# The first loads in parts, the second tile's transposes inside the first chunk, and 26 small products ahead of them

## The chip, the cores and the metric

The kernel runs on one core of a Trainium2 chip. TensorE (PE in the rows, with PEld for its weight loads) does the matrix products and transposes, VectorE (DVE), ScalarE (ACT) and GpSimd (POOL) work on their results, and SyncE (SP) issues nearly all the DMAs. The metric is device time in microseconds for one whole execution, the median of several runs. All data are 32-bit floats.

## What is computed

The reference is two transformer blocks in a row over 256 tokens of 1024 numbers: four layers of one kind, then two of another with experts. What matters here is the very first operation on `x`, the projection of layer 0, and the memory's norm beside it:

```
def first_block(x, mem, ...):
    mem_n = layer_norm(mem, mem_ln_g, mem_ln_b)
    for i in range(DEPTH):
        if kind == 0:
            q, k, v, qi, wi, ki, qm = split_cols(x @ w_in_a[j], ...)
            ki = apply_rope(layer_norm(ki, ...))
            mix = dsa_attention(q, k, v, qi, wi, ki)
        ...
        mk, mv = jnp.split(mem_n @ w_mem_kv[i], 2, axis=-1)
```

`x @ w_in_a[0]` is 256 x 1024 times 1024 x 3144. Everything else in the kernel comes after it.

## The kernel before

The 256 tokens are two tiles of 128 rows (`x[:, 0, :]` and `x[:, 1, :]`). A product takes an activation transposed to 128 x 128 blocks (`xT`) as its stationary operand and a stretch of weights, up to 512 columns wide, as its moving operand. A product of 32-bit numbers shows in the trace as two records, each with a weight load of its own; a transpose is one record.

Weights stream through `ring`, 12 slots of 1 MB each. SP issues loads in the order of the program text; `slot()` makes it wait until the slot's last user is counted in `slots_used`, and each load counts up `slot_full[s]`. The projection is cut into chunks of columns (`FIRST_CHUNKS`): the first is 512 wide (columns 2304 to 2815), the second 328, the third 512. A 512-wide chunk is two slots: rows 0 to 511 of the weights and rows 512 to 1023, which is `k` = 0 to 3 and `k` = 4 to 7 of the eight 128-row blocks.

SP's program (L690 to L697) begins with `ident` (the identity for the transposes), `x` tile 0, `x` tile 1, the two slots of the first chunk, then the memory rows `memrows`, the causal mask, two small constants, and from there the second chunk on. Nothing holds these back but the issue itself: the first wait for a free slot comes at the thirteenth.

TensorE's program for this part is: wait for `ident` and tile 0 (`x_loaded`), eight transposes of tile 0, wait for tile 1, eight of tile 1, each four of them (`transposes`, L994) into one of two PSUM banks `trp`, from which ScalarE copies them to `xT` (L2058). Then `linear_chunk` for each chunk: for each slot, four products of tile 0 and four of tile 1 into two banks of `lin` (L827 is the helper that issues every product), and a count on `slots_used` after each slot. ScalarE copies the finished pair of banks out (L2049). The third chunk has the transposes of the normalised memory between its quarters (`memory_columns`), which wait on `ln_done` from VectorE; VectorE's norm of the memory starts when the gain and bias (`in_mem_ln_g`, `in_mem_ln_b`) have landed. VectorE's first instruction is a memset of `ones` (L3435), which counts up `dve_step`.

In the rows, `sco` is another pair of PSUM banks, first used by the index scores of layer 0.

Of the kernel before, what the change touches and what calls it, by code (L numbers as in the profile page):

```python
# [15 lines left out]
P = 128  # L16
D = 1024
SEQ = 256
NT = SEQ // P
KD = D // P  # L20
# [6 lines left out]
HEADS, DH = 12, 64  # L27
# [36 lines left out]
SLOT = 2048  # L64
# [110 lines left out]
class Tally:  # L175
# [10 lines left out]
    def next(self, k=1):  # L186

        self.n += k
        return self.value()
# [32 lines left out]
def build(nc, A, out):  # L222
    ctx = ExitStack()
    with ctx:
        def sem(name):
            return ctx.enter_context(nc.semaphore(name))
# [199 lines left out]

        slot_full = [sem(f"slot_full{s}") for s in range(X_PLACE + 1)]
        slots_used = sem("slots_used")
        x_loaded, second_tile_loaded, input_loaded = sem("x_loaded"), sem("second_tile_loaded"), sem("input_loaded")
        proj_done = sem("proj_done")  # L430
        tr_full, tr_done = sem("tr_full"), sem("tr_done")
# [117 lines left out]
        def _(sp):  # L549
# [16 lines left out]
            def load_chunk(w, c, n, per=4):  # L566
                K = w.shape[0]
                per = min(per, K // P)
                for k in range(0, K // P, per):
                    load(slot(), 0, per * n,  # L570
                         w[k * P:(k + per) * P, c:c + n].rearrange("(k p) n -> p k n", p=P))
# [116 lines left out]

            sp.dma_start(ident[:, :], const("ident")).then_inc(x_loaded, 16)  # L690
            sp.dma_start(x[:, 0, :], A["x"][0, 0:P, :]).then_inc(x_loaded, 16)
            sp.dma_start(x[:, 1, :], A["x"][0, P:2 * P, :]).then_inc(second_tile_loaded, 16)
            load_chunk(A["w_in_a"][0], *FIRST_CHUNKS[0][0])
            sp.dma_start(memrows, A["mem"][0].rearrange("(t p) d -> p t d", p=P)).then_inc(input_loaded, 16)
            sp.dma_start(causal[:, :, :].rearrange("p t k -> p (t k)"), const("causal")).then_inc(input_loaded, 16)
            sp.dma_start(inv_freq, const("inv_freq")).then_inc(input_loaded, 16)
# [94 lines left out]
        def _(pe):  # L791
# [23 lines left out]
            def slot(loads=1):  # L815
                s = place[0] % RING
                place[0] += 1
                pe.wait_ge(slot_full[s], full[s].next(16 * loads))
                return s
# [123 lines left out]
            def linear_chunk(srcT, K, n, after_each=None, fresh=False):  # L943

                kt = K // P
                per = min(4, kt)
                pair = 2 * (lin_items[0] % 2)
                lin_items[0] += 1
                if t_proj.due():
                    pe.wait_ge(proj_done, t_proj.value())  # L950
                for k0 in range(0, kt, per):
                    s = slot()
                    w = ring[:, s, 0:per * n].rearrange("p (k n) -> p k n", k=per)
                    for t in range(NT):
                        if fresh and (k0 == 0 or t == NT - 1):
                            await_transposes(0 if k0 else (3, 1)[t])
                        for k in range(per):
                            last = mm(lin[:, pair + t, 0:n], srcT[:, k0 + k, t * P:(t + 1) * P], w[:, k, :],
                                      start=k0 + k == 0, stop=k0 + k == kt - 1)
                        if t == NT - 1:  # L960
                            last.then_inc(slots_used, 1)
                        if after_each is not None:
                            after_each()
# [23 lines left out]
            def transposes(pieces, free_slots=0):  # L987

                b = tr_items[0] % 2
                tr_items[0] += 1  # L990
                if t_tr.due():
                    pe.wait_ge(tr_done, t_tr.value())
                for j, src in enumerate(pieces):
                    ins = nc.tensor.transpose(trp[0:src.free_size(), b, j * P:(j + 1) * P], src, ident[:, :])  # L994
                    if j == len(pieces) - 1:
                        ins.then_inc(tr_full, 1)
                    elif free_slots:
                        ins.then_inc(slots_used, 1)
                        free_slots -= 1
                assert not free_slots  # L1000
# [844 lines left out]
                combine_half(1)  # L1845
                t_y.skip(2 * NT)

            pe.wait_ge(x_loaded, 16 * 2)
            for t in range(NT):
                if t:  # L1850
                    pe.wait_ge(second_tile_loaded, 16)
                for b in range(0, KD, 4):
                    transposes([x[:, t, (b + j) * P:(b + j + 1) * P] for j in range(4)])
            for layer in range(FIRST_LAYERS):
                kind = kind_of(layer)
                proj = projA if kind == 0 else projBC
# [1 line left out]
                widths = [n for _, n in FIRST_CHUNKS[kind]]  # L1858
                if layer == 0:
                    memory_left = memory_columns()  # L1860
                    for c, n in enumerate(widths[:3]):
                        linear_chunk(xT, D, n, (lambda: next(memory_left)) if c == 2 else None, c == 0)
                    hold(2)
                    for _ in memory_left:
                        pass
                    linear(memT, D, 512, True)
                else:
                    await_transposes()
                    linear_by_tile(xT, D, widths[:2], lambda: x_columns(1, 1))
                    linear_chunk(xT, D, widths[2])  # L1870
# [1716 lines left out]
```

## Time and profile before

| | us |
|---|---|
| median of 3 runs | 2934.1 |
| lowest and highest | 2932.8, 2934.61 |
| the profiled execution | 2932.43 |
| its span, first to last instruction | 2930.6 |

The profiled execution is 1.7 us below the median. TensorE is busy for 89% of the span. The rows below are from this one execution; times in them are microseconds from the start of the span unless marked ns. In a timeline row the first number is the start, the second the stretch covered, then the engine, the line, the operation, what is written and read, the count of instructions merged in it, and in brackets how long the engine was idle before and what released it.

### The profile page before, as it was taken

How to read it: one execution, taken by the hardware profiler on the slowest of the kernel's cores; microseconds unless marked ns; L12 is line 12 of the kernel's file. 1: busy time of each engine (PE TensorE's matmuls, PEld its weight loads, DVE VectorE, ACT ScalarE, POOL GpSimd, SP SyncE). 2: the span in 40 equal slices, each digit the busy share in tenths (PEclk: the TensorE clock that was granted, in tenths of full speed). 3: DMA queues.
4: the chain of work that ended last, by engine and by line, in shares of the span. 5: the costliest groups of instructions: out<-in, count | busy, mean ns of one | idle time of the engine just before them, and what ended most of it. 6: DMA issues, size and time to landing. Idle time of an engine off the chain costs nothing.

```text
span 2930.6 us, 36560 instructions
## 1 busy us (share of the span) xinstructions
PE 2594.1 (89%) x15534; PEld 1596.4 (54%) x15534; DVE 1193.0 (41%) x2460; ACT 393.7 (13%) x736; POOL 219.9 (8%) x218
## 2 busy tenths in 40 slices
PE   8999999999999999999998999666668999766665
PEld 4569745895559944698457664222224665222221
DVE  2667625675166744777465103001002533100111
ACT  1410002100131001300022111000000412000000
POOL 1110012000120001200011000000000310000000
PEclk9999999999999999999997999878888999888888
DMA  8344543543535435354424557999999455999998
GB/s 310 115 146 165 179 143 112 188 172 136 194 102 187 175 132 172 102 181 178 136 83 146 187 206 280 421 421 421 422 421 379 144 213 183 421 421 421 422 421 342
DMA packets 243719, 703.50 MB, mean 240 GB/s; under 512 B 18795, under 2 KB 119657, under 8 KB 195171
## 3 DMA queue, kind: packets, MB, share of 16 engines
q1 hardware_dynamic: 242256, 699.30, 63.3%
q8 instruction: 126, 2.06, 0.3%
q10 hardware_dynamic: 1299, 1.83, 0.2%
q14 instruction: 38, 0.31, 0.0%
HBM read 698.20 MB, written 1.05 MB: 239 GB/s over the span
## 4 chain that ended last, share of the span: by engine, by line
PE 69%; DMA 21%; SPq 3%; issue 3%; DVE 2%; ACT 1%; POOL 0%; DVEq 0%; POOLq 0%; ACTq 0%
PE lin L827 44%; PE sco L827 14%; PE trp L827 9%; DMA ring<-in_moe_w_up 4%; DMA ring<-in_moe_w_gate 4%; DMA arena<-in_moe_w_down 3%; DMA ring<-in_moe_w_down 3%; DMA spare<-in_moe_w_gate 3%; SPq L663 3%; DMA spare<-in_moe_w_down 2%; PE trp L994 1%; DMA spare<-in_moe_w_up 1%; DMA arena<-in_moe_w_gate 1%; PE trp L1082 1%; DMA ring<-in_xa_wkv 0%
## 5 line engine op out<-in xcount | busy, mean ns | idle before, releaser
L827 PE MATMUL lin<-ring,arena 128*128 128x512 f32 (+4 forms) x2244 | 825.9, 578 | 18.7 <-DMA ring<-in_moe_w_down 8.8
L827 PEld LDWEIGHTS lin<-ring,arena 128*128 128x128 f32 (+1 forms) x2244 | 359.5, 177 | 396.4 <-issue 379.7
L827 PE MATMUL sco<-ring,arena 128*32 128x512 f32 (+2 forms) x1380 | 308.4, 812 | 170.9 <-DMA ring<-in_moe_w_up 52.3
L827 PE MATMUL lin<-arena 128*128 128x128 f32 (+9 forms) x2984 | 356.4, 355 | 28.8 <-DMA arena<-in_moe_w_down 11.2
L827 PE MATMUL sco<-arena 128*32 128x512 f32 (+7 forms) x1832 | 304.8, 457 | 72.9 <-DMA ring<-in_moe_w_gate 26.3
L3350 DVE TENSOR_TENSOR arena<-arena,sco 128x512 f32<-128x512 f32 x16 | 11.0, 688 | 723.7 <-PE sco L827 723.7
L827 PEld LDWEIGHTS lin<-arena 128*128 128x128 f32 (+4 forms) x2984 | 227.0, 162 | 124.1 <-issue 103.8
L827 PEld LDWEIGHTS sco<-ring,arena 128*32 128x32 f32 (+1 forms) x1380 | 84.5, 150 | 339.5 <-issue 337.3
L827 PEld LDWEIGHTS sco<-arena 128*32 128x32 f32 (+4 forms) x1832 | 142.2, 164 | 190.3 <-issue 185.5
L2502 POOL TENSOR_TENSOR roots<-roots 128x1 f32<-128x1 f32 (+2 forms) x42 | 59.7, 1423 | 2332.7 <-DVE roots L2613 2302.7
L827 PE MATMUL lin<-arena,ring 128*128 128x128 f32 (+2 forms) x1672 | 226.6, 301 | 0.0
L827 PE MATMUL trp<-arena 128*128 128x128 f32 (+2 forms) x1520 | 218.1, 299 | 0.6 <-DVE arena L3330 0.6
L827 PEld LDWEIGHTS lin<-arena,ring 128*128 128x128 f32 (+1 forms) x1672 | 207.2, 188 | 14.6 <-issue 3.6
L827 PEld LDWEIGHTS trp<-arena 128*128 128x128 f32 (+1 forms) x1520 | 176.7, 191 | 40.4 <-issue 40.4
L827 PE MATMUL sco<-arena,ring 128*128 128x128 f32 (+1 forms) x1172 | 139.4, 275 | 2.2 <-DVE arena L3282 1.4
L827 PEld LDWEIGHTS sco<-arena,ring 128*128 128x128 f32 x1172 | 135.2, 192 | 5.5 <-DVE arena L3282 3.1
L827 PE MATMUL sco<-spare,arena 128*32 128x512 f32 (+2 forms) x224 | 117.3, 677 | 7.5 <-DMA ring<-in_moe_w_gate 6.0
L2827 DVE TENSOR_TENSOR arena<-ring 128x512 f32<-128x512 f32 x132 | 88.1, 694 | 71.3 <-PE sco L827 70.4
L2058 ACT ACTIVATE arena<-trp 128x512 f32<-128x512 f32 (+1 forms) x115 | 63.2, 590 | 372.5 <-PE trp L994 372.4
L2831 DVE TENSOR_TENSOR ring<-ring 128x512 f32<-128x512 f32 x132 | 89.0, 701 | 1.5
L827 PE MATMUL lin<-spare,arena 128*128 128x512 f32 (+1 forms) x184 | 86.1, 614 | 3.2 <-DMA ring<-in_moe_w_down 3.2
L2833 DVE TENSOR_TENSOR arena<-ring,arena 128x512 f32<-128x512 f32 x132 | 87.8, 692 | 0.0
(337 smaller groups left out, 2285.0 us busy)
## 6 DMA issues: line engine op xcount, KB each, us to landing
ring<-in_w_gate_up SPq DMA_DIRECT2D x88, 1024.0 KB, 5.4
ring<-in_moe_w_up SPq DMA_DIRECT2D x87, 1024.0 KB, 26.7
ring<-in_moe_w_gate SPq DMA_DIRECT2D x75, 1024.0 KB, 27.0
arena<-in_moe_w_down SPq DMA_DIRECT2D x57, 1024.0 KB, 27.0
ring<-in_moe_w_down SPq DMA_DIRECT2D x53, 1024.0 KB, 27.3
ring<-in_w_down SPq DMA_DIRECT2D x44, 1024.0 KB, 5.3
arena<-in_moe_w_gate SPq DMA_DIRECT2D x40, 1024.0 KB, 23.0
arena<-in_moe_w_up SPq DMA_DIRECT2D x31, 1024.0 KB, 27.0
```

Of the source, the lines that this page charges most:

```text
L663: sp.dma_start(dst, src).then_inc(slot_full[s], 16)
L827: return nc.tensor.matmul(o, lhsT, rhs, start=start, stop=stop, skip_group_check=not one_group)
L994: ins = nc.tensor.transpose(trp[0:src.free_size(), b, j * P:(j + 1) * P], src, ident[:, :])
L1082: last = nc.tensor.transpose(trp[:, e, to:to + P], pair_P[j % 3][:, e, lo:lo + P], ident[:, :])
L2058: nc.scalar.activation(dst, trp[0:rows, b, 0:n].rearrange("p (a b) -> p a b", a=shape[1]), ACT.Copy, scale=scale).then_inc(tr_done, 1)
L2502: nc.gpsimd.tensor_tensor(root_out[:, b, 0:n], root_in[:, b, 0:n], root_power[:, 0:n], ALU.pow).then_inc(root_done, 1)
L2827: V.tensor_tensor(first, w12, w11, ALU.subtract).then_inc(dve_step, 1)
L2831: V.tensor_tensor(w12, w22, w12, ALU.subtract)
L2833: ins = V.tensor_tensor(second, w22, first, ALU.subtract)
L3350: V.tensor_tensor(pair_h, pair_silu, sco[:, 1, :], ALU.mult).then_inc(h_done, 1)
```

## The change

SP's first loads are split and put in another order; TensorE's first chunk is written out by hand. In words:

- Tile 0 of `x` comes in two halves of 512 columns, with a semaphore for each (`x_loaded`, `x_rest_loaded`).
- The first weight slot comes in two halves of two row blocks, the first of them (`first_weights_loaded`) ahead of tile 1 of `x`, the second behind it. Two more DMAs are issued than before; the bytes are the same.
- TensorE first waits for VectorE's memset of `ones` and then does 26 products of `ones` with `ones`, 64 columns out of 64, into `sco`; nobody reads them.
- The eight transposes of tile 0 follow, in two groups of four, each behind its half. Then two products of tile 0 (k = 0, 1), the eight transposes of tile 1, two products of tile 0 (k = 2, 3), four of tile 1, and the second slot as before.

```
-            sp.dma_start(x[:, 0, :], A["x"][0, 0:P, :]).then_inc(x_loaded, 16)
+            sp.dma_start(x[:, 0, 0:512], A["x"][0, 0:P, 0:512]).then_inc(x_loaded, 16)
+            sp.dma_start(x[:, 0, 512:D], A["x"][0, 0:P, 512:D]).then_inc(x_rest_loaded, 16)
+            first_column, first_width = FIRST_CHUNKS[0][0]
+            first_rows = [A["w_in_a"][0][256 * h:256 * h + 256, first_column:first_column + first_width].rearrange("(k p) n -> p k n", p=P)
+                          for h in range(2)]
+            s = slot()
+            sp.dma_start(ring[:, s, 0:1024].rearrange("p (k n) -> p k n", k=2), first_rows[0]).then_inc(first_weights_loaded, 16)
             sp.dma_start(x[:, 1, :], A["x"][0, P:2 * P, :]).then_inc(second_tile_loaded, 16)
-            load_chunk(A["w_in_a"][0], *FIRST_CHUNKS[0][0])
+            load(s, 1024, SLOT, first_rows[1])
+            load(slot(), 0, SLOT, A["w_in_a"][0][512:D, first_column:first_column + first_width].rearrange("(k p) n -> p k n", p=P))
...
-            pe.wait_ge(x_loaded, 16 * 2)
-            for t in range(NT):
-                if t:
-                    pe.wait_ge(second_tile_loaded, 16)
+            def first_chunk(n):
+
+                def product(t, k):
+                    return mm(lin[:, t, 0:n], xT[:, k, t * P:(t + 1) * P], w[k // 4][:, k % 4, :], start=k == 0, stop=k == KD - 1)
+
+                def input_columns(t, b):
+                    transposes([x[:, t, (b + j) * P:(b + j + 1) * P] for j in range(4)])
+
+                t_proj.due()
+                lin_items[0] += 1
+                pe.wait_ge(dve_step, 1)
+                for _ in range(26):
+                    mm(sco[0:DH, 0, 0:DH], ones[:, :], ones[:, :])
+                pe.wait_ge(x_loaded, 16 * 2)
+                input_columns(0, 0)
+                pe.wait_ge(x_rest_loaded, 16)
+                input_columns(0, 4)
+                w = [ring[:, s, 0:4 * n].rearrange("p (k n) -> p k n", k=4) for s in range(2)]
+                pe.wait_ge(first_weights_loaded, 16)
+                await_transposes(1)
+                for k in range(2):
+                    product(0, k)
+                pe.wait_ge(second_tile_loaded, 16)
                 for b in range(0, KD, 4):
-                    transposes([x[:, t, (b + j) * P:(b + j + 1) * P] for j in range(4)])
+                    input_columns(1, b)
+                assert slot() == 0
+                for k in range(2, 4):
+                    product(0, k)
+                await_transposes(1)
+                for k in range(4):
+                    last = product(1, k)
+                last.then_inc(slots_used, 1)
+                assert slot() == 1
+                for k in range(4, KD):
+                    product(0, k)
+                await_transposes()
+                for k in range(4, KD):
+                    last = product(1, k)
+                last.then_inc(slots_used, 1)
...
-                    for c, n in enumerate(widths[:3]):
-                        linear_chunk(xT, D, n, (lambda: next(memory_left)) if c == 2 else None, c == 0)
+                    first_chunk(widths[0])
+                    linear_chunk(xT, D, widths[1])
+                    linear_chunk(xT, D, widths[2], lambda: next(memory_left))
```

TensorE's instructions at the very start, before, with the semaphores that each waits for in brackets (one row for a product, which is two records of the trace):

```order
L994 MATMUL trp<-ident,x 128x128 [waits x_loaded]
L994 MATMUL trp<-ident,x 128x128 x7
L994 MATMUL trp<-ident,x 128x128 [waits tr_done,second_tile_loaded]
L994 MATMUL trp<-ident,x 128x128 x3
L994 MATMUL trp<-ident,x 128x128 [waits tr_done]
L994 MATMUL trp<-ident,x 128x128 x3
L827 MATMUL lin<-ring,arena 128x512 [waits tr_done,slot_full0]
L827 MATMUL lin<-ring,arena 128x512 x3
```

And now:

```order
L835 MATMUL sco<-ones 64x64 [waits dve_step]
L835 MATMUL sco<-ones 64x64 x25
L1002 MATMUL trp<-ident,x 128x128 [waits x_loaded]
L1002 MATMUL trp<-ident,x 128x128 x3
L1002 MATMUL trp<-ident,x 128x128 [waits x_rest_loaded]
L1002 MATMUL trp<-ident,x 128x128 x3
L835 MATMUL lin<-ring,arena 128x512 [waits tr_done,first_weights_loaded]
L835 MATMUL lin<-ring,arena 128x512
L1002 MATMUL trp<-ident,x 128x128 [waits tr_done,second_tile_loaded]
L1002 MATMUL trp<-ident,x 128x128 x3
L1002 MATMUL trp<-ident,x 128x128 [waits tr_done]
L1002 MATMUL trp<-ident,x 128x128 x3
```

The first product now stands behind tile 0's transposes and half of the first slot alone; tile 1's transposes have moved behind the second product, and the 26 unread products stand ahead of all.

SP's DMAs at the start, before:

```order
L690 DMA ident<-in_consts 128x128
L691 DMA x<-in_x 128x1024
L692 DMA x<-in_x 128x1024
L564 DMA ring<-in_w_in_a 128x4x512 x2
L694 DMA arena<-in_mem 128x2x1024
```

And now:

```order
L691 DMA ident<-in_consts 128x128
L692 DMA x<-in_x 128x512
L693 DMA x<-in_x 128x512
L698 DMA ring<-in_w_in_a 128x2x512
L699 DMA x<-in_x 128x1024
L565 DMA ring<-in_w_in_a 128x2x512
L565 DMA ring<-in_w_in_a 128x4x512
L702 DMA arena<-in_mem 128x2x1024
```

A quarter of the first chunk's weights has moved ahead of tile 1. From there on both engines' programs, and those of the other three, read as before.

## Rows read from the trace of the kernel before

**Rows 1.** The page: span, engines, and two lines of the 40 slices.
```profile
span 2930.6 us, 36560 instructions
PE 2594.1 (89%) x15534; PEld 1596.4 (54%) x15534; DVE 1193.0 (41%) x2460; ACT 393.7 (13%) x736; POOL 219.9 (8%) x218
...
PEclk9999999999999999999997999878888999888888
GB/s 310 115 146 165 179 143 112 188 172 136 194 102 187 175 132 172 102 181 178 136 83 146 187 206 280 421 421 421 422 421 379 144 213 183 421 421 421 422 421 342
```
**Rows 2.** TensorE's waits in the first 150 us: total, times, longest.
```profile
PE trp L994 <- DVE arena L3507: 2.1, 1, 2.1
```
**Rows 3.** The timeline of the first 30 us, all engines.
```profile
0.83 0.11 DVE L3435 MEMSET ones<- 128x64 f32 x1 [0.83 <-PEq L3573]
...
1.65 0.43 SPq L692 DMA_DIRECT2D x<-in_x  x1
2.13 0.98 SPq L564 DMA_DIRECT2D ring<-in_w_in_a  x2
...
5.13 3.83 PE L994 MATMUL trp<-ident,x 128*128 128x128 f32 x16 [5.13 <-DMA x<-in_x]
...
6.28 0.60 ACT L2058 ACTIVATE arena<-trp 128x512 f32<-128x512 f32 x1 [4.25 <-PE trp L994]
...
9.14 21.04 PE L827 MATMUL lin<-ring,arena 128*128 128x512 f32 x54 [0.17 <-DMA ring<-in_w_in_a]
...
24.14 1.02 ACT L2049 ACTIVATE arena<-lin 128x1024 f32<-128x1024 f32 x1 [14.55 <-PE lin L827]
```
**Rows 4.** TensorE's weight loads, the timeline of the first 26 us.
```profile
10.16 0.33 PEld L827 LDWEIGHTS lin<-ring,arena 128*128 128x128 f32 x1 [0.52 <-issue]
11.01 0.25 PEld L827 LDWEIGHTS lin<-ring,arena 128*128 128x128 f32 x1 [0.52 <-issue]
11.50 0.19 PEld L827 LDWEIGHTS lin<-ring,arena 128*128 128x128 f32 x1 [0.24 <-issue]
```
**Rows 5.** Tile `x`, 0 to 12 us: its DMAs from issue to landing.
```profile
DMA to landing us min/median/max: 3.9/4.3/4.7
```
**Rows 6.** Tile `ring`, 0 to 14 us: its DMAs from issue to landing.
```profile
DMA to landing us min/median/max: 7.0/11.2/12.3
```
**Rows 7.** TensorE's timeline, 1540 to 1556 us (the second block's first mixer).
```profile
1546.98 3.65 PE L827 MATMUL lin<-arena 64*64 64x64 f32 x64 [4.93 <-DVE arena L3141]
```
**Rows 8.** Windows there: stretch, busy time and count by engine, granted clock, DMA share, GB/s.
```profile
1548.00:1550.00 2.00, 2.00 (x42) 2.00 (x40) 1.97 (x4) 0.60 (x1) 0.06 (x1) 0.50 0.03 8
1550.00:1551.00 1.00, 1.00 (x30) 1.00 (x30) 1.00 (x2) 0.31 (x1) 0.00 (x0) 0.73 0.00 0
...
1592.00:1606.00 14.00, 14.00 (x219) 13.81 (x216) 6.67 (x14) 4.30 (x8) 2.01 (x1) 0.50 0.32 117
```
**Rows 9.** TensorE's groups by shape in 1592 to 1606 us: busy, mean ns, idle before.
```profile
L827 PE MATMUL trp<-arena 64*64 64x64 f32 x64 | 7.7, 312 | 0.0
```
**Rows 10.** The timeline of 24 to 110 us, all engines.
```profile
26.92 1.29 DVE L2627 BATCH_NORM_STATS2 small<-arena 128x6 f32<-128x512 f32 x2 [25.98 <-DMA ring<-in_mem_ln_b]
...
34.98 1.28 DVE L2641 SCALAR_TENSOR_TENSOR arena<-arena,roots,ring 128x1024 f32<-128x1024 f32 x1 [0.53 <-POOL roots L2502]
...
40.51 7.03 PE L827 MATMUL lin<-ring,arena 128*128 128x512 f32 x16
...
47.38 1.04 PE L994 MATMUL trp<-ident,arena 128*128 128x128 f32 x8
...
48.26 13.90 PE L827 MATMUL lin<-ring,arena 128*128 128x512 f32 x32
...
50.90 0.23 ACT L2400 ACTIVATE small<-small 128x32 f32<-128x32 f32 x1
...
64.27 1.09 PE L994 MATMUL trp<-ident,arena 128*128 128x128 f32 x8 [2.11 <-DVE arena L3507]
```
**Rows 11.** The chain that ended last, 1790 to 1900 us: start, length, what.
```profile
1829.90 6.29 SPq L663
```

More of the change, by code:

```diff
@@ L428, in build @@
         slots_used = sem("slots_used")
+        x_rest_loaded, first_weights_loaded = sem("x_rest_loaded"), sem("first_weights_loaded")
         x_loaded, second_tile_loaded, input_loaded = sem("x_loaded"), sem("second_tile_loaded"), sem("input_loaded")
```

## The prediction

> **What bounds the kernel now.** I read the page first, then TensorE's waits, then the timeline of the first 30 us, since the change touches nothing behind the first chunk. TensorE is busy for 89% of the span, and the DMAs run at their ceiling of 421 GB/s in two late stretches, the experts' weights [rows 1]. Between the first load and 150 us TensorE waits for something else only once for more than a microsecond, 2.1 us on VectorE at 64.27 [rows 2, 10]. So in the first stage TensorE's own stream sets the pace, and a microsecond won there is won for all that follows, if that one wait moves along.
>
> The start itself: tile 0 lands at 5.13 and 16 transposes run from there to 8.96; the first product starts at 9.14, its weights issued at 2.13 with a landing time of 7.0, so 9.13 [rows 3, 6]. The two slots are 16 products, 32 records. ScalarE takes the bank at 24.14 [rows 3], and since ScalarE began on the first four transposes about 0.2 behind their end (5.13 + 4 x 0.24 = 6.09, against 6.28), the chunk ends on TensorE at about **23.95**. That is the number which the change can move.
>
> How fast these records go: the weight loads start 0.85 apart at 10.16 and 11.01, then 0.49, then 0.43 from 11.50 [rows 4]. The load for a record starts when the one before it does, so TensorE went at 1.2 GHz until about 11.1 and at 2.4 GHz from then on. The page's clock line shows 9 in its first slice and hides this [rows 1]. Counted back from the end, 32 x 0.428 = 13.7 against the 14.8 that it took from 9.14: the slow clock cost 0.9, and 0.2 are the first record's weight load. The 16 transposes at 3.83 / 16 = 0.24 each are slow ones too; later eight take 48.26 - 47.38 = 0.88, or 0.11 each [rows 10].
>
> **The change part by part.** I work out when the first chunk ends.
>
> Loads. The bytes are the same in another order. Ahead of tile 1's landing before stood 64 + 512 + 512 KB, and it landed at 1.65 + 4.7 = 6.35 [rows 3, 5]. The same 1088 KB stand now up to the first quarter of weights: it lands at about **6.35**. Tile 0's second half lands where tile 0 did, 5.13, its first half before that. Tile 1 lies halfway between 6.35 and 9.13, at 7.7, and the rest of slot 0 at 9.13 as before. Slot 1 is another 1 MB: before it was issued at about 2.6, and even with the longest landing time, 12.3 [rows 6], it would be there at 15, before its first use below. SP issues two DMAs more, 0.45 each; the later loads stand behind a queue that takes 7 to 12 us to drain, so 0.9 of issue is hidden. If the cover were gone, the second chunk's weights would be 0.9 later, and TensorE needs them only at 22.
>
> The 26 small products. VectorE's memset ends at 0.94 [rows 3], so they start at about 1.15. They are 52 records of a form that the trace does not have. The nearest is the 64x64 group in 1592 to 1606 us: 7.7 / 64 = 0.12 each at the granted clock 0.50, which is 1.2 GHz [rows 8, 9]. At 2.4 GHz half of that, 0.06. The bounds: 52 x 0.06 = 3.1 us, all fast, and 52 x 0.12 = 6.2, all slow. I take 0.11 for a slow one (a transpose with double the columns is 0.24) and 0.055 for a fast one. Until 5.13 they run in time in which TensorE waited; what runs past that delays the transposes, and so they are not free.
>
> Do they bring the clock up? A burst of 64x64 records that began at 1546.98 after 4.9 us of idleness ran at 0.50 and got the full clock inside 1550 to 1551; a mean of 0.73 there puts it at 1550.5, **3.6 us** after the first record [rows 7, 8]. At the start of the kernel it took 5.95 us from the first transpose, or 1.9 from the first product [rows 3, 4]. Take the first: clock up at 4.75, 33 records done, 19 x 0.055 = 1.0, end at 5.8. Take the second: 7.1, all records slow, end at 6.9. I take the middle, 6.4.
>
> Then the transposes of tile 0, fast: four take 0.45, and ScalarE's copy adds 0.2 + 0.60 + 0.15 as before (its copy ends at 6.88). The first product starts 1.4 behind the end of the small ones: 7.8 (7.2 and 8.3 at the ends). By then the first quarter of weights has been there for over a microsecond. From the first product on the work is 32 x 0.428 = 13.7 and tile 1's eight transposes, 0.9, with no wait in it: tile 1 is there at 7.7 and needed at 9.5, the rest of slot 0 is there at 9.13 and needed at 10.4, slot 1 is needed at 15.5. ScalarE's copies of tile 1 lie beside products 3 and 4. The end is 7.8 + 14.6 = **22.4** (21.8 and 22.9), against 23.95: a gain of **1.6 us** (2.15 and 1.1).
>
> What of this reaches the end. The second chunk needs no wait (above). In the third, the memory's transposes need VectorE's norm, which starts by the DMA's landing at 26.92, not by TensorE, and ends at 34.98 + 1.28 = 36.3; TensorE takes the second tile in the middle of the stretch from 40.51, at 43.9 [rows 10]. 7.6 us of slack swallow no gain. The wait of 2.1 us at 64.27 ends a chain that starts with TensorE: its transposes at 47.38, ScalarE's copies and then its sine at 50.90, VectorE's rotation and norm of the keys [rows 10]. All of it moves along. At the experts, SP waits for a slot that TensorE frees (6.29 us at 1829.90 [rows 11]) just ahead of the long stretch at 421 GB/s, so that stretch begins earlier as well. I carry the whole gain.
>
> The sum: the profiled execution's 2932.43 less 1.6 is 2930.8; the median lies 1.7 above the profiled one, so 2934.1 - 1.6 = **2932.5**.
>
> **The rivals.** *The small products do not raise the clock, and TensorE starts its products later than before.* For it: in 1592 to 1606 us TensorE ran 64x64 records without a gap, 219 in 14 us, and the granted clock stayed at 0.50, while the burst that got 1.00 had 42 records in 2 us, a third more per microsecond [rows 8]. The unread products at 0.11 a record are thinner than either, but each works on twice the area of a 64x64 record. And the 16 transposes at the start did not raise it either; it came 1.9 into the 512-wide products. The Trainium skill says the same of transposes in "TensorE: Matmul & The Clock Gate", Part 4, PE-mode transpose: they don't count as busy in the way products do. By that rule moving tile 1's transposes behind the second product speaks against the change. Price, from rows alone: small ones end at 6.9, transposes slow, first product 6.9 + 0.96 + 0.95 = 8.8; the clock comes 1.8 later, at 10.6; four records take 2.6, the transposes 0.9, and 28 fast records 12.0: end at 24.3, **0.35 slower, 2934.5**. If the transposes between also reset the rise, four records cost 3.4, the transposes 1.9, and 28 records 12.0 + 0.9, from a start at 9.3: 27.5, or 3.6 slower, 2937.7. It decides where start plus slow loss passes 9.4, that is, if the clock has not risen by about 10 us.
>
> *The weights bound it.* If the small products cost less than taken (fast soon, and under 0.055), the first product goes at 6.45 with the first quarter of weights: end at 21.0, a gain of 2.9, 2931.2. Against it: the slow rate of the nearest form.
>
> *The gain is given back at the experts.* The experts' weights pass at 421 GB/s [rows 1], and if that stretch began by something other than a freed slot, nothing would be left: 2934.1. Against it the wait in [rows 11].
>
> *It does something else far away.* The clock also falls and rises in later stages by TensorE's gaps (0.50 in 1592 to 1606), and a shift of a microsecond or two could move such a point by a few microseconds either way. Nothing in the rows gives it a sign.
>
> **How the numbers follow.** Forecast, gain of 0.8 to 2.4: 0.50, with a range of its own of 2931.7 to 2933.3. Clock not raised: 0.22. Weights bound: 0.10. Given back: 0.10. Something else: 0.08. The range takes in the weights-bound case less the spread of a median (the three runs lie 1.3 below and 0.5 above theirs), and goes into the first rival until about one in ten is left on that side: 2930.0 to 2935.8. A measurement of this kernel can tell about 0.2%, 5.9 us, from no change, and no case but the last and the far end of the first comes near that. Faster by more than that 0.04, within it 0.92, slower 0.04.
>
> **What would show it.** In the changed kernel: the products into `sco` from about 1.15, 52 records, their pitch 0.11 and then half; the first product into `lin` at 7.2 to 8.3 (8.8 or later in the first rival, 6.5 in the second); weight loads 0.43 apart from the first product on, where the rival has four or more at 0.85; ScalarE's first copy out of `lin` at 22.6 instead of 24.14; VectorE's first norm still at 26.9; TensorE's wait on VectorE still 2.1 long, at 62.7; and the same distance from there to the end. The prediction is wrong if the copy out of `lin` comes early and the end does not, or if the pitch of the small records is not near 0.11.

## The result: 9 us slower, and the start is not where they went

| | before | after |
|---|---|---|
| median, us | 2934.47 (8 runs) | 2943.72 (8 runs) |
| lowest and highest | 2932.8, 2935.7 | 2941.32, 2944.67 |
| the profiled execution | 2932.43 | 2943.7 |
| its span | 2930.6 | 2941.8 |

The ratio is 1.0031, with a 95% interval of 1.0021 to 1.0041: slower by 9.25 us, where the forecast was faster by 1.6 and the range ended at 2935.8. No run of after lies inside the range.

The page of the profile of after, against [rows 1]; the last line is a DMA queue with packets, megabytes and share:

```profile
span 2941.8 us, 36666 instructions
PE 2598.0 (88%) x15586; PEld 1598.0 (54%) x15586; DVE 1191.2 (40%) x2460; ACT 393.4 (13%) x736; POOL 219.7 (7%) x218
...
q8 instruction: 127, 2.08, 0.3%
```

TensorE is no busier by anything like 9 us. The instruction queue `q8` carries the engines' code; before it had 126 packets and 2.06 MB, now 127: each packet is 16384 bytes.

The start first. The timeline of after from 0 to 30 us, against [rows 3]:

```profile
0.99 5.11 PEld L835 LDWEIGHTS sco<-ones 128*64 128x64 f32 x52 [0.99 <-DVE ones L3478]
...
6.17 1.09 PE L1002 MATMUL trp<-ident,x 128*128 128x128 f32 x8
...
7.73 1.98 PE L835 MATMUL lin<-ring,arena 128*128 128x512 f32 x4 [0.46 <-DMA ring<-in_w_in_a]
...
10.42 19.96 PE L835 MATMUL lin<-ring,arena 128*128 128x512 f32 x56
...
22.69 1.02 ACT L2092 ACTIVATE arena<-lin 128x1024 f32<-128x1024 f32 x1 [11.42 <-PE lin L835]
...
28.21 1.29 DVE L2670 BATCH_NORM_STATS2 small<-arena 128x6 f32<-128x512 f32 x2 [27.27 <-DMA ring<-in_mem_ln_b]
```

ScalarE's first copy out of `lin` comes at 22.69, where it stood at 24.14 [rows 3]: in this pair of executions the start gains 1.45, about what was foreseen. The loss is not here.

To find where it is lost, I took VectorE's instructions of the two traces in their order, the same operation beside the same, and read how much later each starts. This table is worked out from the two traces, one execution of each:

| start in before, us | after minus before, us |
|---|---|
| 51.16 | -1.45 |
| 74.17 | +0.25 |
| 1521.11 | -0.08 |
| 1643.90 | +0.79 |
| 2233.57 | +0.77 |
| 2239.40 | +7.51 |
| 2913.55 | +7.8 |
| 2919.40 | +11.19 |
| 2927.43, near the end | +11.19 |

Three small steps, and two large ones that each lie within six microseconds of before: 6.7 near 2237 and 3.4 near 2917, the ends of the two layers with experts. (The executions that the spans belong to lie 11.2 apart, more than the medians: the profiled one of before is 2.0 below its median of 2934.47, that of after is at its own.) TensorE's timeline of after around the first of them, and the chain that ended last from 2236 to 2247 (start, length, what):

```profile
2237.73 1.12 PE L835 MATMUL sco<-causal,ident 128*128 128x512 f32 x2
...
2244.74 2.08 PE L835 MATMUL lin<-arena 128*128 128x512 f32 x2 [5.89 <-issue]
```

```profile
2237.80 1.06 PE sco L835 x2
2238.85 5.89 issue
2244.74 2.93 PE lin L835 x3
```

"Issue" means that nothing the profile records released the engine: it had no data to wait for, and did not go on. The same view at the second place, in before and then in after:

```profile
2916.93 1.06 PE sco L827 x2
2917.99 0.19 issue
2918.18 1.14 PE lin L827 x2
```

```profile
2924.70 1.06 PE sco L835 x2
2925.76 3.62 issue
2929.38 1.14 PE lin L835 x2
```

```profile
L1823 PEldq COMPARE_BRANCH  x2: 363/402/441, 2237.8 to 2917.7; - x2
```

```profile
L1831 PEldq COMPARE_BRANCH  x2: 3864/4998/6133, 2238.5 to 2925.5; - x2
```

The two jumps take 363 and 441 ns before, 6133 and 3864 ns after: 5.77 and 3.42, together **9.19 us**, beside the 9.25 between the medians. Same line, same operands, same jump over the same 331 instructions (counted in the program: 80 products of four and 11 others). What the engine waits for shows in the DMA queues of after, from 2238.6 to 2242.1 and from 2242.1 to 2243.4:

```profile
q1 hardware_dynamic: 540, 1.39, 104.0%
```

```profile
q1 hardware_dynamic: 218, 0.49, 98.7%
q8 instruction: 1, 0.02, 5.4%
```

For 3.6 us after the jump only data move, at 398 GB/s; then one packet of code is fetched (from 2242.17, by its record), and 2.6 us later TensorE goes on. At the second jump the code transfer starts 1.5 us after it, and TensorE goes on 2.5 later. So the theory: TensorE's code comes in blocks of 16 KB, taken as 256 instructions of 64 bytes, and a jump whose target is not in what has been loaded waits for a transfer. Whether it is loaded depends on where the jump stands in its block, and that depends on how many instructions the program has ahead of it. The change adds 104: each small product is two records of two instructions (load and product), and 26 x 4 = 104. The rest of the edit (halved loads, order) adds none to TensorE but a few waits. The Trainium skill has the mechanism in "Runtime: NRT & Kernel Launch", section Instruction fetch mechanics: code is refilled in 16 KiB blocks of 256 instructions, and a taken branch whose target lies outside the current two-page window forces a fetch before execution goes on. The trace agrees, and adds the price: 5.8 and 3.4 us here.

### The profile page after: what moved, and what is told of

Its sections match the earlier page's. It is cut to its first block, busy times and chain, and to the rows that moved or that the text cites. A ratio compares the mean times of both kernels' runs of the same rounds, so it can differ in the third digit from the quotient of the medians.

```text
span 2941.8 us, 36666 instructions
## 1 busy us (share of the span) xinstructions
PE 2598.0 (88%) x15586; PEld 1598.0 (54%) x15586; DVE 1191.2 (40%) x2460; ACT 393.4 (13%) x736; POOL 219.7 (7%) x218
## 3 DMA queue, kind: packets, MB, share of 16 engines
q1 hardware_dynamic: 242416, 699.30, 62.7%
## 4 chain that ended last, share of the span: by engine, by line
PE 70%; DMA 21%; SPq 3%; issue 3%; DVE 2%; ACT 1%; POOL 0%; DVEq 0%; POOLq 0%; ACTq 0%
PE lin L835 45%; PE sco L835 14%; PE trp L835 9%; DMA ring<-in_moe_w_gate 6%; DMA ring<-in_moe_w_up 5%; DMA arena<-in_moe_w_down 3%; DMA spare<-in_moe_w_down 2%; SPq L664 2%; DMA spare<-in_moe_w_up 2%; PE trp L1002 1%; DMA ring<-in_moe_w_down 1%; DMA arena<-in_moe_w_up 1%; DMA x<-in_moe_w_up 1%; PE trp L1090 1%; SPq L669 0%
## 6 DMA issues: line engine op xcount, KB each, us to landing
arena<-in_moe_w_gate SPq DMA_DIRECT2D x40, 1024.0 KB, 23.2
arena<-in_moe_w_up SPq DMA_DIRECT2D x31, 1024.0 KB, 26.9
```

## The experiments

The rivals to this theory: that the small products do the harm as work (the clock, their place in the start), or the earlier pace does, by shifting loads against each other (my "something far away"), or the new order of loads. In what follows "jumps" are the two durations of the branch instruction in the order of the run, in us. Positions are counted from the program: 4 instructions for a product, 2 for a transpose, 1 for others. By this count the two jumps of before stand at 77 and 42 of a block of 256, up to one unknown constant for what is loaded ahead of the kernel; it is the same for all kernels, and the traces give it further down.

### The small products left out, and alone

```
 e1_no_small: after, without
-            for _ in range(26):
-                mm(sco[0:DH, 0, 0:DH], ones[:, :], ones[:, :])
...
 e2_small_alone: before, with
+            pe.wait_ge(dve_step, 1)
+            for _ in range(26):
+                mm(sco[0:DH, 0, 0:DH], ones[:, :], ones[:, :])
             pe.wait_ge(x_loaded, ...)
```

> The changed kernel without the 26 small products; loads in parts and the new order stay. TensorE's program is then one instruction longer than before the change, not 104. Code-position theory (the 104 extra instructions push the targets of TensorE's two jumps over the overflow path out of what has been fetched): both COMPARE_BRANCH records back at 0.36 and 0.44 us from 6.13 and 3.86, 2933 to 2935 us. Rival, time-shift theory (the new order of loads and transposes moves the work in time, and the experts' stage with its clock and slots answers badly): still 2941 to 2944, with the long branches. First chunk: first product at about 6.5 with the first quarter of weights, slow clock for about 1.9 us, ScalarE's copy at 22.4 to 23.2.

> The kernel before with the 26 small products ahead of its transposes and nothing else. Code-position theory: 104 instructions more, both branches long (6 and 4 us), 2942 to 2945. Time-shift theory: the loads and the order are as before and the first chunk ends within 1.5 us of where it did, so 2932 to 2936. Start: small products end at 6.2 as in the changed kernel, clock up by 5.4 or later, transposes 6.2 to 8.0, first product at 9.1 at the full clock, ScalarE's copy at about 23.1, 1 us earlier than before.

e1 ran 2934.71 (ratio 1.0003, 0.9993 to 1.0012), with jumps of 0.36 and 0.96. e2 ran 2943.97 (1.0034, 1.0022 to 1.0046), with jumps of 6.09 and 3.31. The loss comes with the small products; of the loads and the order none can be seen. (For the start e1 missed: ScalarE's copy was expected at 22.4 to 23.2 and came at 24.77.)

### The same warming with few instructions

```
 e3_wide: after, with
-            for _ in range(26):
-                mm(sco[0:DH, 0, 0:DH], ones[:, :], ones[:, :])
+            for _ in range(4):
+                mm(sco[0:DH, 0, 0:416], ones[:, :], ones[:, 0:1].to_broadcast([P, 416]))
```

> The changed kernel with 4 unread products of 416 columns in place of 26 of 64: the same 1664 columns, so the same time in the array (5.2 us), but 16 instructions in place of 104. Code-position theory: branches short, the start as in the changed kernel (copy of the first chunk at 22.7), 2932.5 to 2934.5, the best of the kernels. Time-shift theory: the start is the changed kernel's to a tenth, so 2941 to 2944.

Four wide products pass as many columns as the 26, in 16 instructions. They covered 5.48 us, where the 26 covered 5.11:

```profile
1.00 5.48 PE L835 MATMUL sco<-ones 128*64 128x416 f32 x8 [1.00 <-DVE ones L3478]
...
8.38 1.98 PE L835 MATMUL lin<-ring,arena 128*128 128x512 f32 x4 [0.88 <-DMA ring<-in_w_in_a]
```

e3 ran 2935.4 (1.0005, 0.9996 to 1.0015), jumps 0.46 and 0.35. So it isn't the warming, the earlier pace or the busy tensor array: it is the number of instructions, or something that goes with it. The 2932.5 to 2934.5 that I expected was missed by 0.9; part of that is a wait of 1.38 behind the first jump, read below.

### Instructions alone

Instructions that do no work, far behind the start, in the loop over the experts' products of the first of the two expert layers (`layer == 0` there) and so ahead of both jumps; in the traces they run between 1897 and 2086 us. They are waits on a semaphore that has long passed, of which two become one instruction.

```
 e4_code_alone: before, with (ahead of parts = expert_parts(4))
+                            if layer == 0 and i in (3, 4) and gate_or_up == 1 and half == 0:
+                                for _ in range(104):
+                                    pe.wait_ge(dve_step, 1)
 e5_more_code: after, with range(90)    (104 + 90 = 194 more than before)
 e6_code_256: before, with i in (2, 3, 4, 5) and range(128)    (256 more)
```

> The kernel before with 104 more instructions on TensorE that only wait for what is long there, 52 in each of two rounds of the first experts' stage, ahead of a wait of 4 us for weights; nothing else. About 50 ns each, 2.6 us a place, inside that wait. Code-position theory: both branches long, 2941 to 2945 with the start unchanged. Time-shift theory: nothing moves, 2934 to 2935.5.

> The changed kernel with all its 26 small products, and 90 more waits that are long met (45 instructions in each of two rounds of the first experts' stage, ahead of a 4 us wait for weights): 194 instructions more than before the change. Code-position theory: if code comes in blocks of 256 instructions, as the steps of about 256 records between the code queue's transfers say, then 194 more put both branches early into the next block, whose successor holds the target. Both branches short again and about 2934 us: the slow kernel gets 9 us faster by more instructions. Rival, amount theory (more instructions on TensorE mean more code to fetch, and that costs): longer than the changed kernel, 2944 to 2952.

> The kernel before with 256 more instructions that wait for what is long there, 64 in each of four rounds of the first experts' stage. 3.2 us a place inside waits of about 4 us; some may show. Code-position theory: the position within a block is that of before, both branches short, 2934 to 2938. Amount theory: two and a half times the 104 of the earlier run that cost 10 us, so 2955 or more.

e4 is the one that settles it: before, with 104 idle instructions and nothing else, ran 2944.2 (1.0033, 1.0021 to 1.0045), the time of after. The branch of e4, and under it that of e6:

```profile
L1826 PEldq COMPARE_BRANCH  x2: 3324/4698/6073, 2241.2 to 2927.9; - x2
```

```profile
L1826 PEldq COMPARE_BRANCH  x2: 362/762/1162, 2240.1 to 2920.2; - x2
```

The idle instructions cost nothing where they stand: by VectorE's starts the shift of e4 against before is 3.38 at 1644 us, ahead of them, and 3.44 at 2234, behind them; that of e6 is 2.32 and 2.34.

e6, with a whole block of 256, is back at 2933.8 (0.9999, 0.9990 to 1.0009): not the count of instructions, but the place in the block. e5, with 194, I expected to be past the bad stretch at both jumps. It was past at one:

```profile
L1834 PEldq COMPARE_BRANCH  x2: 459/2016/3574, 2236.6 to 2917.7; - x2
```

First jump 0.46, second 3.57, and the time between: 2937.49 (1.0011, 1.0002 to 1.0020). The size missed, since the long stretch is wider than I had it; the mechanism gains by it, as each jump switches by itself.

### Where the long stretch begins and ends

```
 e7_code_64: as e4 with range(64)     (64 more than before)
 e8_code_80: as e4 with range(80)     (80 more)
 e12_code_176: before, with i in (2, 3, 4, 5) and range(88)    (176 more)
```

> The kernel before with 64 such waiting instructions, 32 in each of two rounds. Code-position theory: the jump passes over 331 instructions; the target is out of the block after the branch's own from about 181 into a block on. From the counts between code transfers and branch (84 records in the kernel before, 199 to 205 in the changed one) the branches stand at about 148 here: short, 2933 to 2937. If the count of records runs behind the sequencer, the first branch may be long already, 2940. Time-shift and amount theories have no step here: a little over the kernel before.

> The kernel before with 80 waiting instructions, 40 in each of two rounds. Counted by the program, the branches stand at 157 and 122 in their blocks of 256 (77 and 42 before). So far, branches at 15 to 106 were short and at 141 to 236 long. Position theory: the first long (6 us), the second tells the limit: short if it lies above 122. One long: 2940 to 2941; both: 2944.

> The kernel before with 176 waiting instructions, 44 in each of four rounds. The branches stand at 253 and 218. The jump passes 331 instructions, so by position alone a branch at the very end of its block has its target in the block after next: both long, 2943 to 2946. If the block in which the branch stands counts by a few tens of instructions later than the program's own count, the first may be short: 2938.

e7 ran 2941.16 with jumps of 6.11 and 0.37; e8 2942.0 with 6.09 and 3.48; e12 2937.19 with 0.46 and 3.54. One execution each, so here the jumps count, not the times. The branch of e7 and of e12:

```profile
L1826 PEldq COMPARE_BRANCH  x2: 373/3242/6111, 2239.2 to 2926.2; - x2
```

```profile
L1826 PEldq COMPARE_BRANCH  x2: 464/2002/3539, 2238.4 to 2919.3; - x2
```

In e7 the first jump started at 2239.2 and took 6111 ns; in e12 the first took 464 ns. Both limits that I had expected were off: at 64 more the first jump is already long, at 176 more it is short again. All points by place in the block:

| place of the jump, of 256 | jump, us | from |
|---|---|---|
| 15 | 0.46 | e5 first |
| 42 to 43 | 0.43 to 1.16 | before, e1, e6, e10, e11 second |
| 58 to 101 | 0.35 to 0.46 | before, e1, e3, e6, e9, e10, e11 |
| 106 | 0.37 | e7 second |
| 122 | 3.48 | e8 second |
| 141 | 6.11 | e7 first |
| 146 | 3.3 to 3.9 | after, e2, e4 second |
| 157 | 6.09 | e8 first |
| 181 | 6.1 | after, e2, e4 first |
| 218 | 3.54 | e12 second |
| 236 | 3.57 | e5 second |
| 253 | 0.46 | e12 first |

One long stretch, from between 106 and 122 to between 236 and 253, in all kernels, whatever else they contain. Its lower limit is set by second jumps alone; its upper limit lies between a second jump that is long and a first that is short.

Where a block begins can be read from other waits. In the dense stage of 64x64 products TensorE waits on issue a few times in every kernel, in before as well (the chain from 1570 to 1600 us):

```profile
1575.85 2.81 issue
1578.66 2.71 PE lin L827 x45
...
1588.36 2.79 issue
1591.15 0.46 PE sco L827 x14
```

I counted TensorE's records up to each of these waits, weight loads and the sequencer's own instructions included. All 46 waits of more than 0.7 us between 1540 and 1600 us, in the fourteen traces, stand at the same remainder of 256, 193 or 194, and all end 2.3 to 2.7 us behind the start of a code transfer. So blocks are 256 instructions long, and in the count of the table above one begins at place 195 or 196.

Two more waits agree with it. In e3 and e9, whose first jumps are the short ones nearest to the long stretch (places 93 and 101), TensorE waits a little way behind the jump, 28 and 20 records on (the chain from 2238 to 2250 us in e3): 93 + 331 + 28 = 101 + 331 + 20 = 452, which is 196 in the block.

```profile
2245.38 1.38 issue
2246.76 3.40 PE lin L835 x15
```

With the boundary at 195 the 28 jumps of the fourteen traces fall into three kinds:

- The target lies two blocks on, places from about 120 to 194: long in all nine (122 to 181).
- The target lies in the next block, and TensorE had entered its own block 7.2 us or more before the jump: short in all seventeen. Two of them, the second jumps of e1 and e6, took 0.96 and 1.16; there a code transfer had begun 1.55 and 1.23 us ahead of the jump, and TensorE went on 2.5 and 2.4 us behind its start. A transfer was merely late.
- The target lies in the next block, but TensorE had entered its own only 2.3 and 4.3 us before (23 and 41 instructions, places 218 and 236): long in both.

So the plain rule, that a block and the next one are loaded, gives the 75 places from about 120 to 194, and the rest, 41 to 58 places behind the boundary, are jumps that come before the next block has landed. The third kind rests on two jumps, and was read from the traces, not tried.

Why the first jump costs 6.1 and the second 3.3 to 3.9 can be read. In every long jump the branch ends 2.4 to 2.6 us after the code transfer's start; that start comes 3.6 us after the first jump, and 0.9 to 1.5 after the second. 3.6 + 2.5 = 6.1, and 1.0 + 2.5 = 3.5. In before, where nobody waits for it, the next code transfer starts 3.6 after the first jump and 1.2 after the second too, so the delay belongs to the place and not to the stall. At the first the data queue runs full, as shown above. That the loads ahead of it delay the code is likely, and wasn't tried.

### The change, put at a harmless place

```
 e10_change_256: after, with i in (2, 3, 4, 5) and range(76)    (104 + 152 = 256 more than before)
 e11_clock_256: after, with range(72), and in layer 0, ahead of the wait on rope_done,
+                for _ in range(2):
+                    mm(sco[:, 0, :], ident[:, :], causal[:, :, :].rearrange("p t k -> p (t k)"))
 (also 256 more)
 e9_keep_clock: e3_wide with the same two products
```

> The changed kernel, 26 small products and all, with 152 waiting instructions in four rounds of the first experts' stage, so that at both branches the code stands exactly 256 instructions further than before the change, one block. Position theory: both branches short as in the kernel with 256 waits alone (0.4 and up to 1.2 us), and what is left is the value of the change itself: 2932 to 2934.5, at most 2 us better than before. If the start's gain is given back by the clock or in the experts' stage: 2934 to 2936.

> As the kernel before it, and two unread products of 512 columns ahead of the index keys' transposes, in TensorE's wait of 2.1 us, with 144 waiting instructions in place of 152, so again 256 in all at both branches. Clock theory: no fall of the clock at 63 to 70 us, 74 us mark 1.0 to 1.5 ahead of before where the one without them may lose 1.7: 2932 to 2934. If that fall is not what takes the gain: no different from the one without.

> The kernel with 4 wide unread products, and two more unread ones of 512 columns just ahead of the transposes of the index keys, where TensorE waits 2.1 us for VectorE at about 61 to 63 us and the clock fell for 3.4 us in the profiles of the changed kernel and of the wide one. Theory that the start's gain was given back there: no fall of the clock near 64, first stage 1.0 to 1.5 ahead of before at 75 us, and 2932 to 2934. Rival, that the gain is lost in the experts' stage, whose clock and waits vary from run to run: 2934 to 2936, as without them.

e10 is the whole change with both jumps at their old places: 2934.42, beside 2933.42 for the runs of before next to it, ratio 1.0001 (0.9992 to 1.0010), jumps 0.46 and 0.43. e11 ran 2932.96, 0.9998 (0.9989 to 1.0007). So without the cost of the jumps the change is within 0.1% of nothing, and the 1.6 that I forecast is too small for these intervals. Not all of its harm is gone in e10 and e11: their padding runs behind 1897 us, so in the 64x64 stage, at 1540 to 1600 us, they are still 104 instructions ahead of before. That is taken up below.

The reason for e11 and e9 is the first small step of the shift table, -1.45 to +0.25 between 51 and 74 us. The busy time and granted clock of after in three stretches (columns: window, PE, PEld, DVE, ACT, POOL busy, PEclk, DMA share, GB/s):

```profile
62.00:63.40 1.40, 0.57 (x5) 0.58 (x6) 0.77 (x2) 0.00 (x0) 1.32 (x2) 1.00 0.59 228
63.50:66.80 3.30, 3.30 (x8) 1.75 (x7) 0.00 (x0) 1.20 (x2) 2.95 (x3) 0.50 1.02 408
66.90:70.00 3.10, 3.10 (x10) 1.37 (x10) 0.00 (x0) 0.38 (x1) 0.00 (x0) 1.00 0.22 89
```

The clock fell to 1.2 GHz at 63.47 for 3.41 us, which costs half of that, 1.7. It followed the wait on VectorE that the forecast named, 2.12 us long:

```profile
62.83 1.40 PE L1002 MATMUL trp<-ident,arena 128*128 128x128 f32 x8 [2.12 <-DVE arena L3550]
```

Before had the same wait [rows 10] and no fall. Eleven of the fourteen kernels had it at 2.11 to 2.14 us; the clock fell behind it in four of them (after, e3, e4, e6) and stayed in seven. In e9 and e11, where the two unread products lie in it, 0.81 and 0.43 of the wait were left and the clock stayed; in e5 it was 0.42 without them. e10 had 2.14 and no fall. So the two products shorten the wait, but the fall that they were to prevent comes in some executions only, and the runs don't tell what decides it. e9 ran 2936.16 (1.0006, 0.9997 to 1.0015), no better than e3 and outside the 2932 to 2934 that I expected, with a stall on issue of its own:

```profile
2243.04 14.64 PE L835 MATMUL lin<-spare,ring 128*128 128x256 f32 x60 [2.38 <-issue]
```

Its jumps are 0.36 and 0.44, and this stands eight products' records behind the first. The code transfer there starts at 2240.5, and TensorE goes on 2.5 us later, as behind a long jump. So a short jump doesn't rule out a wait for the block behind its target: 1.38 us at place 93 (e3), 2.38 at 101 (e9), none at 77 and 78.

## Why the prediction was wrong, point by point

**The step that failed** is "The 26 small products": "Until 5.13 they run in time in which TensorE waited; what runs past that delays the transposes, and so they are not free." That priced them as time on the engine alone. They are also 104 instructions in its program, and these are paid for at two jumps 2.2 and 2.9 ms later, with 9.19 us. The rows that I had chosen held nothing of it: the branch is not counted as busy, took 0.36 and 0.44 in before, and stood in no group.

**The rival "something else far away"** is the one that came, with 0.08, and by the sign that the prediction gave for being wrong: the copy out of `lin` early, and the end not. I had it as a shift of the clock by "a few microseconds either way" and found nothing to give it a sign. It had a mechanism and, with a count of instructions to each jump, could have been seen as a risk: 9 us at about half of all places. Even its sign was in the trace of before. Its two waits on issue in the 64x64 stage stand at records 19137 and 19649, 512 apart, so blocks begin there. The jumps are then 138 and 103 instructions into theirs, and with the target 332 further on both land in the next block; with 104 more they are at 242 and 207, and both targets lie two blocks on, out of reach by the plain rule. What could not be read from before is the price.

**TensorE's own stream sets the pace.** In the first stage it does: the shift of -1.45 at 51 us is the gain of the start, still whole. "I carry the whole gain" is what didn't hold in after, where it was gone by 74 us. In e2 and e11, where the clock didn't fall, shifts of -0.94 and -0.88 at 51 us were still -0.84 and -0.77 at 1521.

**The end of the first chunk.** Forecast 22.4 and ScalarE's copy at 22.6; in after the copy is at 22.69. The pieces behind it:

- Small products: 52 records from 0.99 to 6.10, forecast 6.4. The pitch of 0.11, then half, held.
- The clock: it reached 2.4 GHz at 5.44 in after. In the seven kernels with warming the trace's records of the granted clock have it at 4.05 to 7.02, in the seven without at 7.74 to 13.18. The small products do raise it, and the first rival (not raised, 0.22) fell. It was argued from their thinness against the 64x64 stage; whatever held the clock there was not at work here. Its other argument, that transposes don't raise the clock, doesn't hold either: in e8, whose start is that of before, it rose at 7.74, with nothing but transposes done since 4.60 and the first product at 8.94.

```profile
4.60 3.56 PE L994 MATMUL trp<-ident,x 128*128 128x128 f32 x16 [4.60 <-DMA x<-in_x]
```

- The first quarter of weights: forecast to land at 6.35, by bytes in order. This is the term that was mis-sized. TensorE waited for it in six of the seven kernels with the new order, by 0.46 to 1.57 us, and the first product came between 7.54 and 9.05; in e10:

```profile
9.05 1.98 PE L835 MATMUL lin<-ring,arena 128*128 128x512 f32 x4 [1.57 <-DMA ring<-in_w_in_a]
```

The first product at 7.73 in after agrees with the forecast of 7.8 for a wrong reason: the transposes were done by 7.3 and the weights were late. "Weights bound" came as a mechanism, but at 7.5 to 9.05 where that rival had 6.45, so it takes from the gain in place of adding to it.

How much of the 1.45 is luck: one execution stood against one. In the six kernels whose start is that of before (e8, e6, before, e4, e12, e7) the copy out of `lin` came at 22.98, 23.89, 24.14, 24.72, 25.04 and 25.48, mean 24.4, and the later the clock rose (7.74 to 13.18), the later it came. In the six with change and warming (e5, after, e9, e11, e3, e10) it came at 22.59 to 24.07, mean 23.2. The gain is about 1.2 in the mean where 1.6 was forecast, and the two groups overlap, so that the 1.45 of this pair came near the forecast by luck. The order alone (e1, 24.77) and the warming alone (e2, 23.21) have one execution each and lie inside the spread of the old start, so their shares are not shown.

**VectorE's first norm at 26.9.** It came at 28.21 in after and as late as 29.55 (e5): its gain and bias land later. The slack of 7.6 us took it up, as the prediction had it.

**The wait of 2.1 at 62.7.** It came as said, 2.12 ending at 62.83. What wasn't said is that the clock can fall behind such a wait: it cost 1.7 us in this execution, and the 1.45 were gone by 74 us.

**The 64x64 stage.** The forecast carried the gain through the second block's first mixer without a word. Between 1521 and 1644 us another 0.9 went. This is code as well. TensorE's waits on issue in 1540 to 1600 us are two in before, 5.6 us in all, and four in after, 8.5. In e10, at the end of the same stage:

```profile
1588.52 0.80 issue
1589.32 0.27 PE lin L835
...
1592.43 3.08 issue
1595.51 0.27 PE lin L835 x2
```

The waits stand where a block of 256 begins (above), and with 104 instructions more ahead of the stage one more such place falls into it. The five kernels that have the 26 small products (after, e2, e5, e10, e11) all wait four times for more than 0.7 us, 7.7 to 9.0 in all; the nine without do so two or three times, 5.6 to 6.5 in all, e4, e6, e7, e8 and e12 among them, whose padding comes later. The whole stretch from 1521 to 1644 us took 0.9 to 1.9 us longer than in before in those five, and between 0.8 less and 1.1 more in the other eight, so the price, one or two microseconds, is less sure than the cause. No run pads ahead of this stage; that trial is missing.

The sum, then, for this execution: 1.45 won, 1.7 lost to the clock, 0.9 in the 64x64 stage, 6.7 at the first jump (of which 5.8 are the jump itself) and 3.4 at the second: 11.2 later, as the two spans differ (what else moved, -0.3 ahead of the 64x64 stage and +0.3 in the last layer, cancels). Between the medians it is 9.25, and the jumps alone make 9.19 of them.

## What to carry to other kernels

An instruction that costs nothing where it stands can cost microseconds at a jump behind it, because it moves that jump within its 256-instruction block, and can bring one more block's beginning into a dense stage: when a time far behind an edit changes, read the branch instructions and "issue" in the chain before looking for causes in the work. Compare two kernels that differ in instruction count only at equal places in the block, by padding one with idle waits to the same number modulo 256 ahead of the first place where code is waited for; otherwise the comparison measures the places. If an engine is to be kept busy with unread work, use few wide instructions (here 16 in place of 104 for the same columns).

## What was not expected of the hardware

- A jump of 331 instructions on TensorE costs 0.35 to 0.46 us at most places and 3.3 to 6.1 at others, with the code in transfers of 16384 bytes. The long places run from 106 to 122 up to 236 to 253 of 256. The Trainium skill, "Advanced Engine Details and Errata", section ISA Cache, gives lines of 256 instructions and two of them; by that alone the stretch would be 75 places wide, and the measured one is 114 to 147. The rest are jumps that came 2.3 and 4.3 us after their block was entered, ahead of the next one's landing.
- In a dense stage TensorE waits for code without any jump: 46 waits of 0.8 to 3.5 us in 1540 to 1600 us of fourteen traces, all at the same remainder of 256 in the count of its records.
- The price of a long jump is the time until the code transfer starts (3.6 us where the loads move 398 GB/s, 0.9 to 1.5 at the other place) and 2.4 to 2.6 us from there.
- A short jump was not always 0.4: 0.96 in e1 and 1.16 in e6, both at place 42 or 43, where before had 0.44; each ended 2.4 to 2.5 us behind the start of a code transfer that was already under way.
- Small loads behind one another did not land by their bytes: the first quarter of weights came 1.2 to 2.7 us later than the 6.35 worked out from the order.
- After the same gap of 2.1 us the clock fell in four of eleven profiles, and stayed in the others. It rose during transposes alone in one (e8, at 7.74).
